# Latent attention: the causal block added by TensorE for score rows of every length, not for the short ones alone

## The reference

```
sc = jnp.einsum('bhqd,bhkd->bhqk', q_blk, kt, preferred_element_type=jnp.float32) * scale
q_idx = i * Q_BLOCK + jnp.arange(Q_BLOCK)
mask = k_idx[None, :] <= q_idx[:, None]
p = jax.nn.softmax(jnp.where(mask, sc, -jnp.inf), axis=-1)
return jnp.einsum('bhqk,bhkd->bhqd', p.astype(vt.dtype), vt)
```

## Time and profile before

| | |
|---|---|
| median of three runs | 2721.07 us (2719.39 to 2722.33) |
| the profiled execution | 2720.82 us, of which its span 2718.9 us |
| busy in the span | PE 2638.5 us, PE weight loads 2097.6, DVE 1842.9, ACT 1337.4, POOL 355.1 |
| granted TensorE clock | 0.996 of full speed |
| attention of group 0 and of group 1 | about 304.6 to 384 us and 412 to 491 us of the span |
| long items, as PE works on them | about 332 to 382 us and 439 to 491 us |

### The profile page before, as it was taken

How to read it: one execution, slowest core, us unless ns; L and a number is a source line. 1 busy time by engine, 2 the same in 40 slices (tenths; PEclk the granted TensorE clock), 3 DMA queues, 4 the chain that set the end, 5 groups by cost and what they waited for, 6 DMA issues and landing times.

```text
span 2718.9 us, 33427 instructions
## 1 busy us (share of the span) xinstructions
PE 2638.5 (97%) x13368; PEld 2097.6 (77%) x13368; DVE 1842.9 (68%) x2423; ACT 1337.4 (49%) x1923; POOL 355.1 (13%) x222
## 2 busy tenths in 40 slices
PE   7999999999999999999999999999999899999998
PEld 3577666777888888877888877887778788888877
DVE  5777555578677677795443347544334899999998
ACT  3531868333222333344453356435523577777775
POOL 1000450000000000000000000000000376334333
PEclk9999999999999999999999999999999999999999
DMA  9422200023444956623001130210115899999995
GB/s 334 124 63 62 105 34 1 32 101 124 163 155 150 341 211 238 220 97 135 2 32 47 47 124 1 94 62 1 62 38 207 311 381 381 389 395 393 385 378 218
DMA packets 149362, 451.25 MB, mean 166 GB/s; under 512 B 16762, under 2 KB 50840, under 8 KB 124624
## 3 DMA queue, kind: packets, MB, share of 16 engines
q1 hardware_dynamic: 132944, 419.33, 41.6%
q0 software_dynamic: 16256, 29.71, 3.0%
HBM read 411.21 MB, written 62.93 MB: 174 GB/s over the span
## 4 chain that ended last, share of the span: by engine, by line
PE 78%; DVE 10%; ACT 5%; DMA 4%; issue 2%; SPq 0%; POOL 0%; POOLq 0%; DVEq 0%; ACTq 0%
PE PS L181 73%; PE PS L192 5%; DMA MR_<-in_w_e_up 3%; DVE ML_ L4307 2%; PE PS L649 1%; DVE BIG L508 1%; ACT BIG L1115 0%; DVE ST L514 0%; DMA BIG<-in_w_ada 0%; ACT MLH L4302 0%; DVE WOP L2018 0%; DVE XR L4438 0%; DMA BC<-in_w_ada 0%; ACT BIG L1355 0%; ACT BIG L1346 0%
## 5 line engine op out<-in xcount | busy, mean ns | idle before, releaser
L4307 DVE TENSOR_TENSOR ML_<-MR_,MLH 128x2048 fp32r<-128x2048 f32 x192 | 438.2, 2302 | 28.4 <-ACT MLH L4302 27.3
L4302 ACT CAST MLH<-MR_ 128x2048 fp32r<-128x2048 f32 x192 | 367.4, 1915 | 93.3 <-DMA MR_<-in_w_e_up 39.1
L181 PE MATMUL PS<-MLH,MLX 128*128 128x512 f32 x1024 | 320.7, 394 | 7.5 <-DVE ML_ L4307 5.4
L181 PE MATMUL PS<-BIG 128*64 128x128 f32 (+12 forms) x1616 | 230.2, 347 | 10.9 <-ACT BIG L3472 4.3
L181 PEld LDWEIGHTS PS<-MLH,MLX 128*128 128x128 f32 x1024 | 189.8, 189 | 50.1 <-DVE ML_ L4307 10.4
L181 PE MATMUL PS<-ML_,MLX 128*128 128x512 f32 x512 | 199.9, 390 | 0.0
L181 PEld LDWEIGHTS PS<-BIG 128*64 128x64 f32 (+5 forms) x1616 | 131.4, 162 | 72.0 <-issue 50.8
L181 PE MATMUL PS<-WOP,T4R 128*128 128x512 f32 x672 | 155.0, 389 | 0.5 <-DVE WOP L2290 0.5
L181 PE MATMUL PS<-T1R,T2R 128*128 128x512 f32 x672 | 154.6, 389 | 0.0
L181 PEld LDWEIGHTS PS<-WOP,T4R 128*128 128x128 f32 x672 | 126.0, 188 | 26.8 <-DVE WOP L2290 0.7
L181 PEld LDWEIGHTS PS<-T1R,T2R 128*128 128x128 f32 x672 | 126.1, 188 | 26.2
(11 more groups left out here) (647 smaller groups left out, 5954.1 us busy)
## 6 DMA issues: line engine op xcount, KB each, us to landing
MR_<-in_w_e_gate SPq DMA_DIRECT2D x64, 1024.0 KB, 20.7
MR_<-in_w_e_up SPq DMA_DIRECT2D x64, 1024.0 KB, 21.6
MR_<-in_w_e_down SPq DMA_DIRECT2D x64, 1024.0 KB, 23.4
BIG<-in_w_ff SPq DMA_DIRECT2D x32, 1024.0 KB, 7.3
BIG<-fz SPq DMA_DIRECT2D x28, 1024.0 KB, 4.9
fz<-BIG SPq DMA_DIRECT2D x48, 512.0 KB, 2.7
BC<-in_w_ada SPq DMA_DIRECT2D x32, 512.0 KB, 3.5
BIG<-in_w_ff SPq DMA_DIRECT2D x32, 512.0 KB, 3.7
```

The lines of the kernel that those rows point to most:

```text
L181: ins = pe.matmul(o, l, r, start=(start and n == 0), stop=(stop and n == len(pairs) - 1), skip_group_check=True)
L4302: act.copy(cut_at(MH, i), raw(i)).then_inc(e.w_hi.up(), 1)
L4307: dve.tensor_tensor(low_at(i), raw(i), cut_at(MH, i).bitcast(F32), ALU.subtract).then_inc(e.w_lo.up(), 1)
```

## The change

PE adds the block for every item. The short item's place is as before (bank 2(n mod 2), column 128 i); a long item's diagonal block is in the second bank, at column 128 (i - 4). The semaphore that tells DVE that the scores are there is raised by this product for all items. DVE's addition and its wait go.

```
                             c1 = min(nk, c0 + 512)
                             ins = mm(PS[:, 2 * (n % 2) + c0 // 512, 0:c1 - c0],
                                      [(QT[0:96, h, 128 * i:128 * i + 128], KT[0:96, h, c0:c1])])
-                        if i < 4:
-                            ins = mm(PS[:, 2 * (n % 2), nk - 128:nk], [(C("ident"), C("caus"))], start=False)
+                        b, c0 = 2 * (n % 2) + i // 4, 128 * (i % 4)
+                        ins = mm(PS[:, b, c0:c0 + 128], [(C("ident"), C("caus"))], start=False)
                         ins.then_inc(s_pe.up(), 1)
...
                     if n < NI:
-                        i = ITEMS[n][1]
-                        nk = 128 * (i + 1)
+                        nk = 128 * (ITEMS[n][1] + 1)
                         flat = PS[:, 2 * (n % 2):2 * (n % 2) + 2, :].rearrange("p b n -> p (b n)")
                         bi = smq(n)[1]
-                        d = flat[:, nk - 128:nk]
                         V.wait_ge(*s_pe[n + 1])
-                        if i >= 4:
-                            dve.tensor_tensor(d, d, C("caus"), ALU.add).then_inc(vs.up(), 1)
-                            V.wait_ge(*vs.last)
                         dve.tensor_reduce(bi, flat[:, 0:nk], AX, ALU.max, negate=True).then_inc(bias_ok.up(), 1)
```

## The result

The changed kernel takes 2726.68 us, the median of 14 runs (2722.68 to 2730.66), beside 2720.82 us for 14 runs of the kernel before (2717.49 to 2722.88). The ratio is 1.0022, with a 95% interval of 1.0013 to 1.0030: the change made the kernel slower by 5.9 us.

What follows compares the result with a forecast made beforehand. The prediction took PE to bound the long items' stretch. Products cost 6.6 us, less 0.33 of stall and 0.66 at the tails: +5.6 on 2721.07 makes 2726.7 us, range 2723.9 to 2729.5.

Steps and rivals of the forecast that it cites:

- PE is the bound in the long stretch: While PE works on long items, its matmul rows cover all 43.09 us and the chain of waits stays on PE.
- 0.22 us a product: Each added 128x128 fp32 product, two matmul records between an item's scores and the next transposes, costs PE 0.22 us.
- The lower price: For an added product, the skill's 81 ns per weight load and matmul gives 0.16 us, the whole change 3.8 us.
- 15 of 16 on the path: Each group's first long item hides its product behind ACT's backlog; the other 15 cost, 30 x 0.22 = 6.6 us.
- 0.17 us of stall absorbed in each group: Five early transposes held up by ACT's copy no longer stall: 0.17 + 0.16 = 0.33 us less over both groups.
- 0.33 us from each tail: Behind each group's last item, the maximum starts 0.33 us sooner without DVE's addition: 0.66 us gained in all.
- Everything behind moves along: Everything behind 491 us should be moved by 5.6 us and otherwise be unchanged.
- the second rival: No change: the 5.29 us wait for output weights at 528.16 swallows 5.3 of 5.6 us, 2721.4 us; chance 0.06.
- the first: Faster: the softmax loop sets the long stretch's pace, each of 32 items 0.33 us shorter, 2710.5 us; chance 0.04.
- the third: Slower by more: each product costs its full 0.39 us instead of 0.22, sum 10.7 us, 2731.8 us; chance 0.06.

Runs made afterwards that it cites:

- the second product: Against the changed kernel, PE adds the table's block twice for long items: 2733.91 us, ratio 1.0052 of the kernel before.
- the run with neither: Against the changed kernel, nobody adds the table for long items, neither PE's product nor DVE's addition: 2719.14 us, ratio 0.9996 of the kernel before.
- the placed products: Against the changed kernel, PE's product only for short items, 16 and 31 (group 0), 17 and 18 (group 1), DVE's addition for other long ones: one run, 2715.41 us.
- the first such kernel: Against the changed kernel, the product uses bf16 copies of identity and table for items of all lengths: 2724.09 us, ratio 1.0014 of the kernel before.
- these two kernels: Changed kernel with bf16 product for all items, 2724.09 us; or only for short items, 16 and 31, DVE's addition for other long ones, 2724.48 us.

## Why the prediction was right

The forecast was 2726.7 us against a measured 2726.68, a change of 5.6 against 5.9 us, and slower by over 0.2% was the likeliest of three. The measured ratio of 1.0022 is on that side, with an interval that reaches across the line, as the chances of 0.52 and 0.44 had it. That the medians agree within 0.02 us is luck: the runs after lie 8 us apart, the median before came out 0.25 us below the one that the forecast was added to, and the measured change can be anything from 3.5 to 8.2 us by its interval. What bears the account are the lengths inside the attention, by the prediction's steps:

- **PE is the bound in the long stretch.** Shown by the second product, which cost what the first did, and by the run with neither, whose stretch kept its length.
- **0.22 us a product.** (46.24 - 43.09 + 0.17) / 15 = 0.221 us, and 0.223 for the second one. The lower price by the Trainium skill, "TensorE: Matmul & The Clock Gate", section "Back-to-back issue gap", an estimate of two times 81 ns, is not what fp32 shows here; the bf16 product, one record, cost 0.063.
- **15 of 16 on the path.** Shown by the placed products: item 16 free, item 31 at 0.22 us; and by the kernel after, in both groups.
- **0.17 us of stall absorbed in each group.** Shown by the same run: 0.71 us with the product left out before it, 0.55 with two products.
- **0.33 us from each tail.** 6.69 and 6.68 became 6.35; with the addition put back 6.68 and 6.69.
- **Everything behind moves along.** In the profile the last exponent of group 1 is 4.28 us later than before (484.22 became 488.50), 5.6 less the 1.31 us of head start. The output weights' transfer, which the second rival saw swallowing the delay, was issued 4.28 us later too, 528.16 against 532.44, behind a wait of 152.9 us for PE, where it had been 147.4:

```profile
532.44 0.92 SPq L1451 DMA_DIRECT2D OWR<-in_w_out  x2
```

```profile
SPq L1451 <- PE PS L181: 152.9, 1, 152.9
```

A little was given back all the same: ACT took up the landed weights 5.04 us after the issue, against 5.31 before (533.47), and PE's first product behind them started 4.00 us later than before and not 4.28 (543.18 against 539.18). In the eight other profiles the weights are taken up 5.03 to 5.26 us behind the issue, with the product and without it, so these 0.28 us are put down to the transfer's spread and not to the change.

Of the rivals the first fell by the runs with a second product and with none, the second by these rows, and the third by the price. One sentence held for the median but not for the one profile: that everything behind 491 us should be 5.6 us later. It left out that two executions can start a stage over a microsecond apart, and that a transfer can land a quarter of one sooner, for reasons far from the change.

## What to carry to other kernels

Work moved from an engine with slack to the engine on which the chain of waits lies costs its full pace, start to start, however small it is beside that engine's total. What the relieved engine gains is only what stands on the chain, here the last item of each group. Before such a move, look for the turns in which the busy engine waits anyway (a backlog, a stall, the end of a stage): in this kernel the added work was free or paid there, and nowhere else.

## What had not been expected of the hardware

A cheaper matmul went with a loss of time. Where the short items' product was in bf16, and so one short record instead of two, the granted clock stood at half of full speed for some 10 us in three of four cases, 0.66 in the mean of the windows shown; in the fourth, group 1 of the first such kernel, it stayed at 1.00 though PE's weight loads had gone from 15.84 us in the kernel before to 12.18. The price was 2.5 us in group 0 of that kernel (28.77 against 26.25 us from the first reciprocal to the stretch). The mean clocks of single executions point the same way beyond the profiled ones: 0.991 to 0.995 in the 22 runs of these two kernels, 0.995 to 0.997 in those of the kernel before beside them; 10 us at half the clock take 0.002 off the mean. With the fp32 product there the clock was 1.00 from 300 to 335 us and from 410 to 445 us in every other profile of this study. That PE's lower activity is the cause is the likely reading, but it was not tried by itself, for instance with idle products in place of the saved ones.
